# A 1-core two-block transformer kernel: the first modulation, norm and products taken one input tile at a time

## What is computed

```python
c_act = jax.nn.silu(c)
ada = c_act @ w_ada[l] + b_ada[l]
sh_m, sc_m, g_m, sh_f, sc_f, g_f = jnp.split(ada, N_ADA, axis=-1)
h = modulate(rmsnorm(x, norm_mix_g[l]), sh_m, sc_m)
...
proj = h @ w_in
...
def modulate(hn, shift, scale):
    return hn * (1.0 + scale[:, None, :]) + shift[:, None, :]
```

## Time and profile before

| | |
|---|---|
| time, median of 3 runs | 1012.35 us (1012.17 to 1012.78) |
| time of the profiled execution | 1012.1 us |
| its span | 1010.3 us |
| TensorE busy | 1000.6 us (99%) |
| VectorE busy | 683.6 us (68%) |
| ScalarE busy | 577.5 us (57%) |
| transferred | 196.81 MB, mean 195 GB/s |

### The profile page before, as it was taken

The page is one execution under the profiler, slowest core; times in us unless marked ns, Lnnn a source line. Parts: engine busy times, 40 slices in busy tenths (PEclk is TensorE's granted clock), DMA queues, the critical chain, the costliest instruction groups (busy, mean ns, idle before and its releaser), DMA issues.

```text
span 1010.3 us, 17849 instructions
## 1 busy us (share of the span) xinstructions
PE 1000.6 (99%) x7344; PEld 933.4 (92%) x7344; DVE 683.6 (68%) x1153; ACT 577.5 (57%) x961; POOL 0.4 (0%) x5
## 2 busy tenths in 40 slices
PE   9999999999999999999999999999999999999997
PEld 7899999999999999999999999998999899999996
DVE  5698888878898677887558545455766557555552
ACT  4778665556555456767647544454666446444442
POOL 0000000000000000000000000000000000000000
PEclk9999999999999999999999999999999999999999
DMA  9965767535666545453336555555553327545521
GB/s 383 364 250 182 262 235 287 204 132 210 248 256 246 204 169 189 160 198 126 126 102 230 211 177 198 175 200 183 209 192 126 126 105 254 204 170 204 172 81 42
DMA packets 28016, 196.81 MB, mean 195 GB/s; under 512 B 3104, under 2 KB 3744, under 8 KB 4640
## 3 DMA queue, kind: packets, MB, share of 16 engines
q1 hardware_dynamic: 27360, 194.95, 53.5%
q10 hardware_dynamic: 576, 0.72, 0.2%
HBM read 194.61 MB, written 1.05 MB: 194 GB/s over the span
## 4 chain that ended last, share of the span: by engine, by line
PE 96%; ACT 1%; DVE 1%; issue 0%; ACTq 0%; POOLq 0%
PE PS L996 16%; PE PS L997 16%; PE PS L998 16%; PE PS L1256 8%; PE PS L1257 8%; PE PS L1258 8%; PE PS L1150 3%; PE PS L1153 3%; PE PS L1151 3%; PE PS L1198 2%; PE PS L1200 2%; PE PS L1199 2%; PE PS L1351 2%; PE PS L1340 1%; PE PS L1373 1%; PE PS L1039 1%
## 5 line engine op out<-in xcount | busy, mean ns | idle before, releaser
L1790 DVE TENSOR_TENSOR wlo<-raw,whi 128x1024 fp32r<-128x1024 f32 (+1 forms) x314 | 368.2, 1217 | 111.2 <-ACT whi L1416 110.9
L1416 ACT ACTIVATE whi<-raw 128x1024 fp32r<-128x1024 f32 x308 | 307.0, 1048 | 156.9 <-PE PS L1258 93.4
L996 PE MATMUL PS<-Hh,whi 128*128 128x256 f32 x1232 | 352.5, 286 | 1.3 <-DVE Hl L1764 1.3
L997 PE MATMUL PS<-Hl,whi 128*128 128x256 f32 x1232 | 348.5, 283 | 0.0
L998 PE MATMUL PS<-Hh,wlo 128*128 128x256 f32 x1232 | 348.4, 283 | 0.0
L996 PEld LDWEIGHTS PS<-Hh,whi 128*128 128x128 f32 x1232 | 236.0, 192 | 8.7 <-issue 7.0
L997 PEld LDWEIGHTS PS<-Hl,whi 128*128 128x128 f32 x1232 | 236.2, 192 | 1.4
L998 PEld LDWEIGHTS PS<-Hh,wlo 128*128 128x128 f32 x1232 | 236.1, 192 | 0.0
L1256 PE MATMUL PS<-whi,Oh 128*128 128x512 f32 x344 | 134.6, 391 | 0.0
L1257 PE MATMUL PS<-wlo,Oh 128*128 128x512 f32 x344 | 134.2, 390 | 0.0
L1258 PE MATMUL PS<-whi,Ol 128*128 128x512 f32 x344 | 133.9, 389 | 0.0
(11 more groups left out here) (255 smaller groups left out, 1348.0 us busy)
## 6 DMA issues: line engine op xcount, KB each, us to landing
raw<-wall SPq DMA_DIRECT2D x155, 1024.0 KB, 4.9
raw<-wada SPq DMA_DIRECT2D x18, 1024.0 KB, 5.0
GA<-wada SPq DMA_DIRECT2D x2, 1024.0 KB, 18.6
GA<-alibi SPq DMA_DIRECT2D x1, 2048.0 KB, 9.5
raw<-wall SPq DMA_DIRECT2D x2, 768.0 KB, 5.9
X<-xt SPq DMA_DIRECT2D x1, 1024.0 KB, 5.3
KM<-wada SPq DMA_DIRECT2D x1, 1024.0 KB, 14.4
QF<-wada SPq DMA_DIRECT2D x1, 1024.0 KB, 16.4
```

Of the source, the lines that this page charges most:

```text
L996: e.matmul(dst, wh, a, start=start, stop=False, skip_group_check=share)
L997: e.matmul(dst, wh, b, start=False, stop=False, skip_group_check=share)
L1416: e.activation(whi[place(n)][:, c], raw[i % RAW][:, c], ACT.Copy).then_inc(*up("a_whi", (n, half)))
L1790: e.tensor_tensor(wlo[place(n)][:, c], raw[i % RAW][:, c], f32(whi[place(n)][:, c]), ALU.subtract).then_inc(*up("v_wlo", (n, half)))
```

## The change

- The 2048 columns of w_ada are laid out anew: one 1 MB block holds all 1024 rows of the 128 shift and 128 scale columns of one input tile. `ada_rows`, `ada_columns` and the vector steps run eight times, once for a tile, on half the columns, with eight matmuls of 256 columns where a round had eight of 512.
- The first four weight chunks, and x, are transferred by halves (512 KB) and interleaved with the blocks of w_ada. The split of weights in this stage goes by halves as well, the first half by quarters.
- The sums of squares of x are taken with a 128x128 matrix of ones (`x_total`), so that each partition holds every token's sum. ScalarE takes the root of 128x256, VectorE the reciprocal of 128x256 in place (`x_root`). Spreading by transposes and the copy are gone.
- ScalarE writes `Hh` at once from the normed tile; VectorE makes the unrounded tile `TT` itself, with the same gain and shift, and subtracts.
- In the list the steps of tile i+1 stand among the products of tile i. `ROWS_AFTER` says after how many of its 8 parts `ada_rows` stands; two parts later comes `ada_columns`. The norm of tile i+2 follows. There are 15, 1, 2 and 5 `warm` matmuls where there were 26, 3, 3, 4 and 7.
- `positions` is converted later, out of `COS`; the angle steps are spread over four tiles; the table load for the square root stands after tile 6 and no longer after chunk 4's split.

Cut to its core (a line of "..." marks what is left out):

```diff
+ROWS_AFTER = (3, 2, 1, 0, 0, 0, 0)
...
     emit("silu_c")
+    emit("warm", 15, 0)
+    emit("x_squares")
+    emit("x_total", 7)
+    emit("x_root", 7)
+    emit("warm", 1, 0)
+    emit("ada_rows", 0)
+    emit("mix_norm", 0)
+    emit("warm", 2, 0)
+    emit("ada_columns", 0)
+    emit("first_weights", 0)
+    emit("mix_tile", 0)
+    emit("first_weights", 1)
+    emit("mix_norm", 1)
+    emit("warm", 5, 0)
...
-    for s in range(3):
-        if s:
-            emit("weights", s + 1, s + 1, (0,))
-        emit("slice", s, PARTS[0:5])
-        emit("ada_rows", s + 1, 0)
-        emit("ada_rows", s + 1, 1)
-        if s == 0:
-            emit("angles", 1)
-            emit("weights", s + 1, s + 1, (0,))
-        emit("slice", s, PARTS[5:8])
-        emit("ada_columns", s + 1)
-        emit("slice", s, PARTS[8:16])
-        st["done"] = s
-        tile(2 * s + 2)
-        emit("weights", s + 1, s + 1, (1,))
-        st["have"] = s + 1
-        taken(s + 1)
-        tile(2 * s + 3)
...
+    for i in range(8):
+
+        s, parts = i // 2, [(i % 2, t) for t in range(8)]
+        if i == 6:
+            parts = LAST_PARTS[0:6]
+        elif i == 7:
+            parts = LAST_PARTS[6:16]
+        if i == 7:
+            emit("slice", s, parts)
+            break
+        r = ROWS_AFTER[i]
+        emit("slice", s, parts[0:r])
+        emit("weights", (i + 1) // 2, (i + 1) // 2, ((i + 1) % 2,))
+        emit("ada_rows", i + 1)
+        emit("slice", s, parts[r:r + 2])
+        emit("ada_columns", i + 1)
+        emit("slice", s, parts[r + 2:])
+        if i % 2:
+            st["done"] = s
+        emit("mix_tile", i + 1)
+        if i < 6:
+            emit("mix_norm", i + 2)
+        if i % 2 == 0:
+            st["have"] = s
+            taken(s)
+        if i in (1, 2, 3):
+            emit("angles", i)
+        elif i == 4:
+            emit("tables")
             emit("final_gain")
-        elif s == 1:
-            emit("tables")
-        else:
+        elif i == 5:
             emit("signs")
+            emit("root_table")
+        elif i == 6:
...
-        e.dma_start(X[:, :, :], xt).then_inc(*up("d_x", 0, 16))
+        for half in range(2):
+            e.dma_start(X[:, 4 * half:4 * half + 4, :], xt[:, 4 * half:4 * half + 4, :]).then_inc(*up(f"d_x{half}", 0, 16))
+        e.dma_start(ID[:, :], masks[:, 0:128]).then_inc(*up("d_id", 0, 16))
...
+        load_ada(0)
+        load_half(0, 0)
+        e.dma_start(posi, pos).then_inc(*up("d_pos", 0, 16))
+        load_ada(1)
+        load_half(0, 1)
+        for j in range(2, 8):
+            load_half(j // 2, j % 2)
+            load_ada(j)
...
+            elif step == "x_total":
+
+                b, = a
+                for k in range(4):
+                    on.wait_ge("v_sq", ("x", k // 2))
+                    m = e.matmul(PS[:, b, 0:T], ONES[:, :], SQ[:, k, :], start=k == 0, stop=k == 3)
+                m.then_inc(*up("t_sq", "x"))
+                free[b] = ("a_rb", "x")
...
-                for q in range(4):
+                bank(4 + p % 2)
+                on.wait_ge(f"d_ada{p}", 0)
+                for k in range(8):
+                    q = k % 4
                     m = e.matmul(
-                        PS[32 * q:32 * q + 32, 4 + p % 2, :],
-                        CA[:, 4 * half + q:4 * half + q + 1].to_broadcast([128, 32]),
-                        first_ada[2 * p + half][:, q * 512:q * 512 + 512], start=half == 0, stop=half == 1)
-                if half == 1:
-                    m.then_inc(*up("t_arow", p))
-                    free[4 + p % 2] = ("a_arow", p)
+                        PS[32 * q:32 * q + 32, 4 + p % 2, 0:256], CA[:, k:k + 1].to_broadcast([128, 32]),
+                        first_ada[p][:, k * 256:k * 256 + 256], start=k < 4, stop=k >= 4)
+                m.then_inc(*up("t_arow", p))
+                free[4 + p % 2] = ("a_arow", p)
...
+            elif step == "x_root":
+                b, = a
+                on.wait_ge("t_sq", "x")
+                on.wait_ge("d_small", 0)
+                e.activation(RB[:, 0, :], PS[:, b, 0:T], ACT.Sqrt, bias=col("eps"), scale=1.0 / D).then_inc(*up("a_rb", "x"))
+                sq_free.update({i: ("t_sq", "x") for i in range(4)})
...
-                e.activation(TT[:, i % 2, :], QM[:, i, :], ACT.Identity, scale=GS[:, i:i + 1], bias=ADA[:, i:i + 1]).then_inc(
-                    *up("a_x", i))
-            elif step == "mix_split":
-                i, = a
-                on.wait_ge("a_x", i)
-                e.activation(Hh[:, i, :], TT[:, i % 2, :], ACT.Copy).then_inc(*up("a_xhi", ("mix", i)))
-                tt_free[i % 2] = ("v_xlo", ("mix", i))
+                e.activation(Hh[:, i, :], QM[:, i, :], ACT.Identity, scale=GS[:, i:i + 1], bias=ADA[:, i:i + 1]).then_inc(
+                    *up("a_xhi", ("mix", i)))
...
+            elif step == "x_root":
+                on.wait_ge("a_rb", "x")
+                e.reciprocal(RB[:, 0, :], RB[:, 0, :]).then_inc(*up("v_rec", "x"))
...
-                for at, c in ((2 * p, 0), (8 + 2 * p, 2)):
-                    m = e.tensor_tensor(
-                        ADA[:, at:at + 2], LM[:, c:c + 2], col("b_ada", at, 2), ALU.add)
-                m.then_inc(*up("v_adab", ("first", p)))
-                on.wait_ge("v_adab", ("first", p))
+                e.tensor_tensor(ADA[:, p:p + 1], LM[:, 0:1], col("b_ada", p), ALU.add).then_inc(*up("v_adab", ("first", p)))
                 e.scalar_tensor_tensor(
-                    GS[:, 2 * p:2 * p + 2], ADA[:, 8 + 2 * p:10 + 2 * p], 1.0, col("norm_mix_g", 2 * p, 2),
-                    ALU.add, ALU.mult).then_inc(*up("v_gs", p))
+                    GS[:, p:p + 1], LM[:, 1:2], col("norm_mix_g", p), GS[:, p:p + 1], ALU.mult, ALU.add).then_inc(
+                    *up("v_gs", p))
...
+                is_free(tt_free, i % 2)
+                e.tensor_scalar(
+                    TT[:, i % 2, :], QM[:, i, :], GS[:, i:i + 1], ADA[:, i:i + 1], ALU.mult, ALU.add).then_inc(
+                    *up("v_tile", i))
+                on.wait_ge("v_tile", i)
...
-    first = w[:, 0:2048].reshape(2, 4, 128, 2, 4, 256).transpose(4, 0, 2, 1, 3, 5).reshape(8, 128, 2048)
+    first = w[:, 0:2048].reshape(8, 128, 2, 8, 128).transpose(3, 1, 0, 2, 4).reshape(8, 128, 2048)
     rest = w.reshape(4, 2, 128, 6, 1024).transpose(3, 0, 2, 1, 4).reshape(24, 128, 2048)[8:]
```

More of the change, by code:

```diff
@@ L948, in load, with load_ada, load_half @@
                 e.dma_start(raw[slot][:, 0:n], wall[it[1]][:, 0:n]).then_inc(*up(f"d_raw{slot}", i, 16))
-        for s in range(4):
-            for j in (2 * s, 2 * s + 1):
-                e.dma_start(first_ada[j], wada[j]).then_inc(*up(f"d_ada{j}", 0, 16))
-            load(s)
+        def load_ada(j):
+            e.dma_start(first_ada[j], wada[j]).then_inc(*up(f"d_ada{j}", 0, 16))
+        def load_half(s, half):
+            if s in (2, 3):
+                on.wait_ge("t_arow", s - 2)
+            c = slice(half * CH // 2, (half + 1) * CH // 2)
+            e.dma_start(raw[s][:, c], wall[s][:, c]).then_inc(*up(f"d_first{half}{s}", 0, 16))
+        load_ada(0)
[6 more added lines that the diff above has]
+            load_ada(j)
         e.dma_start(TRI[:, :], masks[:, 128:384]).then_inc(*up("d_tri", 0, 16))
@@ L987, in weights_there @@
         def weights_there(n, last):
+            if n == 0 and last <= CH // 4:
+                on.wait_ge("a_whi", (0, "first"))
+                on.wait_ge("v_wlo", (0, "first"))
+                return
             on.wait_ge(hi_mark(n), (n, (last - 1) // (CH // 2)))
@@ L1044, in tensor @@
                 bank(b)
[L1045 to L1052 removed]
+                if name == "q":
                     on.wait_ge("a_sq", ("q", 2))
@@ L1395, in scalar @@
         on = On(e, marks)
-        x_at = {k: ("d_x", 0) for k in range(8)}
-        sq_free, rb_free, tt_free, pt_free = {}, {}, {}, {}
+        x_at = {k: (f"d_x{k // 4}", 0) for k in range(8)}
+        sq_free, rb_free, pt_free = {}, {}, {}
         def is_free(held, *at):
@@ L1792, in vector @@
                         *up("v_wlo", (n, half)))
+            elif step == "first_weights":
+                c = slice(a[0] * CH // 4, (a[0] + 1) * CH // 4)
+                key = (0, 0 if a[0] else "first")
+                on.wait_ge("a_whi", key)
+                e.tensor_tensor(wlo[0][:, c], raw[0][:, c], f32(whi[0][:, c]), ALU.subtract).then_inc(*up("v_wlo", key))
+            elif step == "silu_c":
+                on.wait_ge("d_small", 0)
+                e.scalar_tensor_tensor(
+                    GS[:, 0:8], col("b_ada", 8, 8), 1.0, col("norm_mix_g", 0, 8), ALU.add, ALU.mult).then_inc(
+                    *up("v_gs", "base"))
             elif step == "ada_columns":
```

105 lines of the change are left out of this document (34 added, 71 removed).

## The result

The changed kernel takes **1016.0 us** (median of 8 runs, 1014.1 to 1016.34), the kernel before beside it 1012.62 (8 runs, 1012.17 to 1012.82): a ratio of 1.0028, 95% interval 1.0019 to 1.0037. It is slower by 3.4 us, where the prediction had 1012.5 and a range up to 1015.2. The profiled execution took 1016.21 with a span of 1014.2.

What follows compares the result with a forecast made beforehand. TensorE's work and waits in the first stage were taken to bound the kernel. Terms -4.5 + 2.4 + 2.1 = 0.0, or +0.2 with all overlaps, took the median from 1012.35 to 1012.5; range 1009.6 to 1015.2.

Steps and rivals of the forecast that it cites:

- first term: Start of the first stage: X's second half at 6.2, reciprocal 2.4, first product at 14.0, 4.5 us earlier.
- rival on half transfers: Transfers of the first stage: halves run slower, deciding from 0.8 us a transfer; time 1020; chance 0.04.
- second term: w_ada rounds on TensorE: seven on the path at 1.43 us each, 10.0 against 7.5 before, 2.4 us more.
- rival of rounds paid by records: w_ada rounds on TensorE cost by records, not columns: 2.0 us a round, +4.4 net, 1016.9; chance 0.12.
- third term: TensorE's waits at tiles 1, 2, 7 and the transposes of tiles 6, 7: 2.95 against 0.87, 2.1 us more.
- rival without waits: First stage: ScalarE's and VectorE's steps overlap better, stage ends 2.1 to 3.0 us earlier, time 1009.5; chance 0.20.
- signs that were to show the prediction wrong: TensorE's waits from the first product on summing under 1 or over 5 us, or a round far from 1.4.
- The fall of the clock: TensorE, idle 1.9 us before the first product, falls from 2.4 to 1.2 GHz; with slow reciprocal 1014.8; chance 0.06.

## Why the prediction was wrong

The changed kernel was to take 0.2 us more and took 3.4. By like runs, without the fall, it is 1014.69 (7 runs) against 1012.1 to 1012.5 by chip: 2.2 to 2.6, which is the stage's 2.5. The rest of the 3.4 is that, by their groups, the clock fell in five of the one set of eight and in none of the other. With the fall the difference is larger, 1016.27 against 1013.1 to 1013.4, 2.9 to 3.2, and that is not explained. The stage ended 2.3 later than the forecast had it: 1.6 of this comes from the first term and 0.8 from the third.

**The first term, the start, is the step that failed.** "X's second half lands about when all of X did", put at 6.2, was read from a transfer of 1 MiB. The half landed at 8.2, and a whole X at 6.4 in the same kernel. The rival on half transfers says "Here each half stands behind others in the same queue"; that holds for the weights and not for X, which stands first but for the small `SM`. The pieces of the chain behind it: VectorE's two operations 1.50 (1.29 taken), the sums until 10.90 (1.0 taken from the second addition, 1.15 measured), the reciprocal 1.76. With 2.4 for it I had erred the other way, by 0.65; neither the extrapolation from 2 and 4 elements nor one pass was right. By the Trainium skill, VectorE: DVE Perf Modes, section "First, the fixed hardware budget", the estimate was 2.1, worked out from its repeat count of 8; the trace has less, 1.76. First product 15.64 for 14.0: 1.6 late. The gain at the start was 2.9, not 4.5.

**The rival of the half transfers** had the right mechanism in the wrong place. I looked for it at the end of the stream, where w_ada of tile 7 lands at 39.4 (38 expected), and nothing waits for it: the stream moves 402 to 434 GB/s from 12 to 42 us in windows of two, 388 to 432 before the change. At the head of the queue nothing is ahead to hide behind: 270 GB/s against 416. The Trainium skill's rule, DMA: Bandwidth & Descriptors, section "Bandwidth", to batch at least 1 MiB, agrees with that place of the trace and would have given this sign; with the stream from 12 to 42 us, which holds the halves of the weights, it does not agree.

**The second term, the rounds, was right.** A round costs 1.20 from product to product, and its transposes 0.22: 9.94 for seven (10.0 predicted). The rival of rounds paid by records, at 2.0, is out.

**The third term, the waits, was right in its places and short in size:** 1.0, 0.65, 0.63, 0.48, 1.01, in all 3.8, for 2.95. The rival without waits is out with it. What was missed is some 0.25 to 0.3 ahead of each of tiles 1, 2 and 7. Of this the traces show 0.09, as `Hl` waits 0.29 for `Hh` and not 0.2, and 0.08, as a product behind a wait has its successor 0.20 later, not 0.12; the rest is a few hundredths at each step (from tile 2's transposes to its first product it is 2.23 for 2.00). The run that moved the rounds took the waits of tiles 1 and 2 away for a gain; the one that moved the tables took those of the columns away, for a wait behind the stage. The signs that were to show the prediction wrong (waits in sum under 1 or over 5, a round far from 1.4) did not come: they looked at the second and third term, and the error was in the first.

**The fall of the clock** was in the rivals, but ahead of the first product, where 1.5 us of idle TensorE brought none. It comes behind the sums in some runs of both kernels. What brings it is not settled. By the runs it is not the new stage, and neither the place in time nor the one-column products on end bring it by themselves. In one profile it came behind a wait of 2.65 us; in another, behind one of 1.49, it did not. The groups lie 0.7 to 1.1 apart in the kernel before and 1.6 in the changed one (1014.69 and 1016.27). The slow products cost 1.4 to 1.5 in a trace of either stage, so the difference is not in their price, and what makes it is open.

## What to carry to other kernels

Price a transfer at the head of a queue apart from the same bytes in the stream, and keep what the first chain needs in one piece: here the second of two halves came 0.5 to 2.2 us later than the whole. When a producer is moved earlier on one engine, look at what its copy now stands in front of on the next; the tables moved last only moved the wait, and a round moved ahead made it longer. Read the times of single runs before a median: a difference of 3.4 held 2.2 to 2.6 of the change, and the rest came with a clock that falls in some runs.

## What the hardware showed that I had not expected

- The granted clock falls to 0.50 for about 3 us behind the sums in some executions (57 to 61 us in the changed kernel, 55 to 59 in one that has the stage of before) and not in others, with TensorE at work all the time.
- Seven kernels with X whole have it at 6.4 to 6.7 us; by halves, in eleven, the second lands between 7.2 and 8.6.
- The reciprocal over 128x256 is 1.75 us, 6.8 ns an element of a partition's row, where 4 elements take 0.175.
- A product of ones with `start` in other columns of a bank in which one-column sums were open changed those sums. It was seen in one kernel and not taken apart.
